# A routed expert layer on one core: the first round starts from what is known beforehand instead of waiting for the round tables

## The reference

```python
w = sel_v / jnp.sum(sel_v, axis=-1, keepdims=True)     # top 2 of the best group of 4
gates = jnp.sum(one_hot(sel_i, 16) * w[..., None], axis=1)
for e in range(16):
    h = silu(x @ w_exp_gate[e]) * (x @ w_exp_up[e])    # 1024 -> 512
    y = y + gates[:, e:e + 1] * (h @ w_exp_down[e])    # 512 -> 1024
```

## Time and profile before

| | us |
|---|---|
| median of 3 runs | 1483.75 |
| lowest and highest run | 1483.48, 1492.34 |
| span of the profiled execution | 1481.6 |
| PE busy (share of the span) | 1413.4 (95%) |
| DVE busy | 598.1 (40%) |
| ACT busy | 273.3 (18%) |

### The profile page before, as it was taken

How to read it: one execution, slowest core, us unless ns; L and a number is a source line. 1 busy time by engine, 2 the same in 40 slices (tenths; PEclk the granted TensorE clock), 3 DMA queues, 4 the chain that set the end, 5 groups by cost and what they waited for, 6 DMA issues and landing times.

```text
span 1481.6 us, 20595 instructions
## 1 busy us (share of the span) xinstructions
PE 1413.4 (95%) x7002; PEld 734.0 (50%) x7002; DVE 598.1 (40%) x1216; ACT 273.3 (18%) x667; POOL 116.8 (8%) x137
## 2 busy tenths in 40 slices
PE   7999998998999999998999999999989999999898
PEld 3787446453344443443457874475543444443344
DVE  5086785545310110106530867844543101101356
ACT  1201335212100100011121013442121101100111
POOL 2100000110000000003000000001100000000300
PEclk9999999999999999999999999988999999999999
DMA  8714003354499999948031240033434999999821
GB/s 298 262 62 155 17 1 118 142 191 155 142 421 426 427 427 426 389 159 291 0 130 58 73 156 5 1 118 142 190 142 143 355 426 427 426 427 427 332 90 47
DMA packets 80941, 319.47 MB, mean 216 GB/s; under 512 B 12684, under 2 KB 15044, under 8 KB 56300
## 3 DMA queue, kind: packets, MB, share of 16 engines
q1 hardware_dynamic: 66772, 272.19, 47.1%
q0 software_dynamic: 9280, 29.68, 5.4%
q10 hardware_dynamic: 4824, 16.75, 2.8%
HBM read 429.21 MB, written 29.67 MB: 310 GB/s over the span
## 4 chain that ended last, share of the span: by engine, by line
PE 82%; DMA 5%; DVE 5%; issue 2%; ACT 2%; SPq 1%; DVEq 1%; POOL 1%; ACTq 0%; POOLq 0%
PE psum L1367 19%; PE psum L957 12%; PE psum L1394 9%; PE psum L1453 8%; PE psum L1025 8%; PE psum L1230 7%; PE psum L927 4%; DMA region<-in_w_exp_up_dram 3%; PE psum L896 2%; PE psum L1368 2%; PE psum L875 2%; PE psum L1281 1%; PE psum L1346 1%; PE psum L1010 1%; PE psum L1047 1%
## 5 line engine op out<-in xcount | busy, mean ns | idle before, releaser
L1367 PE MATMUL psum<-ring,xT 128*64 128x512 f32 x800 | 356.7, 598 | 7.4 <-issue 3.1
L1368 PE MATMUL psum<-region,xT 128*64 128x512 f32 x800 | 357.6, 599 | 0.0
L1367 PEld LDWEIGHTS psum<-ring,xT 128*64 128x64 f32 x800 | 107.4, 138 | 208.8 <-issue 208.7
L1394 PE MATMUL psum<-ring,region 128*64 128x512 f32 x400 | 176.2, 592 | 4.3 <-issue 2.7
L957 PE MATMUL psum<-xT,ring 128*128 128x272 f32 x768 | 176.5, 393 | 0.0
L1395 PE MATMUL psum<-region 128*64 128x512 f32 x400 | 176.3, 593 | 0.0
L957 PEld LDWEIGHTS psum<-xT,ring 128*128 128x128 f32 x768 | 145.8, 190 | 30.1
L2242 DVE COPY region<-psum 128x512 f32<-128x512 f32 x23 | 15.9, 691 | 317.5 <-PE psum L1395 317.5
L1025 PE MATMUL psum<-ring,xT 128*128 128x512 f32 (+1 forms) x288 | 132.5, 603 | 0.6 <-DVE region L1896 0.6
L1453 PE MATMUL psum<-ring,xT 128*128 128x512 f32 x256 | 118.0, 617 | 1.6 <-ACT xT L1495 1.5
L782 POOL TENSOR_TENSOR rr<-rq,half 128x1 f32<-128x1 f32 (+4 forms) x41 | 55.9, 1363 | 723.7 <-DVE rq L1762 267.6
(11 more groups left out here) (286 smaller groups left out, 1464.8 us busy)
## 6 DMA issues: line engine op xcount, KB each, us to landing
region<-in_w_exp_gate_dram SPq DMA_DIRECT2D x54, 1024.0 KB
ring<-in_w_exp_gate_dram SPq DMA_DIRECT2D x54, 1024.0 KB
region<-in_w_exp_up_dram SPq DMA_DIRECT2D x54, 1024.0 KB
ring<-in_w_exp_up_dram SPq DMA_DIRECT2D x54, 1024.0 KB
ring<-in_w_exp_down_dram SPq DMA_DIRECT2D x54, 1024.0 KB
region<-in_w_exp_down_dram SPq DMA_DIRECT2D x54, 1024.0 KB
ring<-in_w_in_dram SPq DMA_DIRECT2D x24, 1024.0 KB, 8.0
expert_results<-region ACTq DMA_DIRECT2D x23, 512.0 KB, 7.7
```

The lines of the kernel that those rows point to most:

```text
L1367: pe.matmul(bank[b][front, :], xeT[:, kc, front], ring[:, BLOCK_SLOT[u], kc % 4, :], start=kc == 0, stop=kc == KC - 1)
L1368: m = pe.matmul(bank[b][last, :], xeT[:, kc, last], back[:, UNIT_ROOM[u], kc % 4, :], start=kc == 0, stop=kc == KC - 1)
L1394: pe.matmul(bank[5 + half][front, :], hT[:, 2 * n + q, front], ring[:, BLOCK_SLOT[u], 2 * q + half, :], start=n + q == 0, stop=n + q == 2)
```

## The change

SP no longer serves round 0 from the tables: the early loads are taken as its weights. The back lane's `down` load moves ahead of the wait for `routed`, and `part_of(gate, 1)` is the first thing that reads the tables. To make that right, experts 0 and 15 always get at least one half tile (`least`, a maximum with 64 rows). The count of rounds done, `base`, is kept in registers by each engine instead of being read from `ctl`, and PE, ACT and DVE wait for `routed` and read `mid` after round 0's rows have been turned and copied. DVE's table arithmetic keeps sizes in rows instead of half tiles, with about as many instructions.

The constants and the table arithmetic:

```diff
-    c["rounds"] = np.stack([r, -1 - r])[None].astype(np.float32)
+    c["rounds"] = np.stack([r, -r])[None].astype(np.float32)
...
+    least = np.zeros(NE)
+    least[[0, NE - 1]] = HALFROWS
...
-                ve.tensor_scalar(R(18, 16, 32), R(18, 16, 32), STEP64, 1.0 / HALFROWS, ALU.subtract, ALU.mult)
+                ve.scalar_tensor_tensor(R(18, 16, 32), R(18, 16, 32), STEP64, tie[:, 32:48], ALU.subtract, ALU.max)
...
-                ve.tensor_scalar(ctl[0:1, 1:2], cumf[0:1, 1:2], -1.0, None, ALU.add)
-                ve.tensor_copy(ctl[0:1, 0:1], cumf[0:1, 0:1]).then_inc(routed, 1)
-                ve.tensor_tensor(cumf[0:1, 0:1], cumf[0:1, 0:1], cumf[0:1, 1:2], ALU.add)
...
+                ve.tensor_scalar(ctl[0:1, 1:2], cumf[0:1, 1:2], -1.0, None, ALU.add).then_inc(routed, 1)
```

SP:

```diff
                 base = rounds_done
+                key = ("pp", 4, 1)
+                hold(full[use(key)], taken(l, key) + 1)
+                hold(xe_full, 16 * (base + 1))
                 for n in range(2):
-                    hold(b_full[BLOCK_SLOT[("gate", n)]], 16 * (base + l + 1))
-                    hold(z_full[BLOCK_SLOT[("gate", n)]], 16 * (base + l + 1))
+                    early("down", n, 1)
                 hold(routed, l + 1)
...
-                for name in ("gate", "up", "down"):
-                    if name == "down":
-                        key = ("pp", 4, 1)
-                        hold(full[use(key)], taken(l, key) + 1)
-                        hold(xe_full, 16 * (base + 1))
-                        part_of("gate", 1)
-                        for n in range(2):
-                            early("down", n, 1)
-                    for n in range(2):
-                        if name != "gate":
-                            hold(b_full[BLOCK_SLOT[(name, n)]], 16 * (base + l + 1))
-                            hold(z_full[BLOCK_SLOT[(name, n)]], 16 * (base + l + 1))
-                    if name != "down":
-                        part_of(name, 0, True)
+                part_of("gate", 1)
...
                 rounds_done = base + mid + 1
-                part_of("down", 0)
                 part_of("up", 1)
```

PE:

```diff
-                pe.wait_ge(routed, l + 1)
-                pe.sem_inc(pe_pass, 1)
-                base = pe.value_load(ctl[0:1, 0:1], min_val=0, max_val=MAXROUND * (DEPTH - 1))
-                mid = pe.value_load(ctl[0:1, 1:2], min_val=MINROUND - 1, max_val=MAXROUND - 1)
-
+                base = rounds_done
...
-                    pe.wait_ge(b_full[s], 16 * (base + l + k + 2))
-                    pe.wait_ge(z_full[s], 16 * (base + l + k + 2))
+                    pe.wait_ge(b_full[s], 16 * (base + k + 1))
+                    pe.wait_ge(z_full[s], 16 * (base + k + 1))
...
                 turn_rows(0)
+                pe.wait_ge(routed, l + 1)
+                pe.sem_inc(pe_pass, 1)
+                mid = pe.value_load(ctl[0:1, 1:2], min_val=MINROUND - 1, max_val=MAXROUND - 1)
+                rounds_done = base + mid + 1
                 gate(0)
```

DVE, after the copy of the turned rows:

```diff
                 rows_half(0)
+
+                ve.wait_ge(routed, l + 1)
+                ve.sem_inc(ve_pass, 1)
+                mid = ve.value_load(ctl[0:1, 1:2], min_val=MINROUND - 1, max_val=MAXROUND - 1)
+                rounds_done = base + mid + 1
```

More of the change, by code:

```diff
@@ L342, in encoder_step @@
         rdec = sb("rdec", [P, 4, 4])
-        tie = sb("tie", [P, 32])
+        tie = sb("tie", [P, 48])
         valid = sb("valid", [P, TILES])
@@ L710, in entry, with part_of @@
                     return e.value_load(ctl[0:1, bass.ds(2 + table * MAXROUND + k, 1)], min_val=lo, max_val=hi)
-                def part_of(name, k, first=False):
+                def part_of(name, k):
                     front = bass.ds(l * NE + entry(0, k, 0, NE - 1), 1)
@@ L720, in part_of @@
                         read = {"gate": (gate_read, gate_full), "up": (up_read, up_full), "down": dn_full}[name][n]
[L721 to L722 removed]
+                        hold(read, base + k + 1)
                         e.dma_start(ring[:, s, :, :], weights(name, n, front), cond=new_front).then_inc(b_full[s], 16)
                         e.dma_start(back[:, UNIT_ROOM[(name, n)], :, :], weights(name, n, last), cond=new_last).then_inc(z_full[s], 16)
[L726 to L739 removed]
+                part_of("gate", 1)
                 e.dma_start(lnp_near[:, 0, :], a["ln2_g"][L].to_broadcast([P, D])).then_inc(ln2p_in, 16)
@@ L908, in _ @@
             pe.wait_ge(ident_bias, 16)
+            rounds_done = 0
             for l in range(DEPTH):
@@ L1676, in _ @@
                     projected(t)
-                sc.wait_ge(routed, l + 1)
-                sc.sem_inc(sc_pass, 1)
-                base = sc.value_load(ctl[0:1, 0:1], min_val=0, max_val=MAXROUND * (DEPTH - 1))
-                mid = sc.value_load(ctl[0:1, 1:2], min_val=MINROUND - 1, max_val=MAXROUND - 1)
+                base = rounds_done
                 def rows_half(k):
@@ L1708, in _ @@
                 rows_half(0)
+                sc.wait_ge(routed, l + 1)
+                sc.sem_inc(sc_pass, 1)
+                mid = sc.value_load(ctl[0:1, 1:2], min_val=MINROUND - 1, max_val=MAXROUND - 1)
+                rounds_done = base + mid + 1
                 silu(0)
@@ L2191, in _ @@
                 ve.drain()
-                ve.tensor_scalar(seat[:, 1, :], rounds[:, 1, :], tiles, cumf[0:1, 1:2], ALU.add, ALU.max)
+                ve.tensor_scalar(seat[:, 1, :], rounds[:, 1, :], rt[0:1, 12, 40:41], cumf[0:1, 1:2], ALU.add, ALU.max)
                 ve.drain()
```

28 lines of the change are left out of this document (13 added, 15 removed).

## The result

The changed kernel takes 1472.79 us (median of 20 runs, 1468.75 to 1483.05) against 1480.53 (20 runs of the kernel before beside it, 1474.64 to 1493.63). The ratio is 0.9948 with a 95% interval of 0.9925 to 0.9971: 0.5% shorter, so a real gain, inside the 1% (14.8 us) that the forecast called what a measurement can tell. Timed again beside other kernels it gave 0.9931 (0.9895 to 0.9967).

A forecast was written before the change was run, and what follows sets the result against it. PE, busy nearly everywhere, was taken to bound the 1481.6 us span. Starts and clock 3.5 (layer 0) and 3.3 us (layer 1) plus SP's lead 4.0 made 10.8: span 1470.8, plus 2.15 to the median, 1473 us; range 1467 to 1480.

The forecast's parts named there:

- signs that the prediction had named itself: Wrong if layer 0's rounds end under 5 or over 8 us earlier, or stretches outside the rounds differ by over 2.
- Transposes earlier: Start of rounds: first transposes no longer wait for PE's two `ctl` reads; 1.8 us in layer 0, 1.6 in layer 1.
- the floor now is the gather: First transposes of each layer: the gathered rows' landing limits their start, so no more than 1.8 and 1.6 us can come.
- The read of `mid`: Behind the first transposes: one read, about 0.95 us, stays hidden on PE, so `gate(0)` starts 1.7 us after the first transpose.
- side sum of 10.9 against 9.9: Total gain in us if the `mid` read is hidden behind queued work (10.9), or if it is not (9.9).
- The clock of `gate(0)`: Shorter rest before the transposes keeps PE's clock up: `gate(0)` 6.9 us instead of 8.6, gain 1.7 us a layer.
- SP's lead: Load queue: SP issues round 2's `gate` 8.8 us earlier in PE's time; worth 4.0 us over both layers, bounds 0 to 8.
- (b): Late rounds: the stretch with full DMA engines starts from a smaller backlog; 2.0 us in layer 0, 1.1 in layer 1.
- (a): Layer 0, `gate(2)`: PE's 0.75 us wait for the load's second half goes, some 0.9 us with the step around it.
- reads in series (2): Start of rounds: register reads do not hide behind the transposes, costing 0.5 us a layer, 1474 us; chance 0.18.
- The clock of another stretch (4): Layer 1, 992 to 1009 us: the low-clock stretch may run up to 7 us shorter, giving 1466 to 1470; chance 0.14.
- The loss of SP's worth (3): Clock falls anyway (1476) or SP's lead is worth nothing, 4.0 us less (1477), both 1480; chance 0.15 in all.

The follow-up runs named there:

- the second profile: The changed kernel, unaltered, profiled a second time: span 1468.2 us, against 1473.9 in its first profile and 1481.6 before the change.
- experiment 6: Changed kernel plus sixteen identity transposes during TensorE's wait for seat tables, and VectorE's `mid` read behind its matrices: 1471.00 us; with the transposes alone 1473.18 us.
- Experiment 1: Changed kernel with SP's load queue put back as before, TensorE again counting round 0's conditional loads, computing engines in the new order: 1483.64 us, ratio to before 1.0028.
- experiment 2: Changed kernel's SP queue kept, but computing engines wait for the tables and read two numbers before the first transposes, as before: 1480.78 us, ratio to before 1.0002.
- Experiment 3: Computing engines changed, load queue as before, but `gate` and `up` of round 0 wait for one signal less: 1481.36 us, ratio to before 0.9989.
- experiment 4: Changed kernel with twelve more table reads on SP ahead of its loop of rounds: 1472.07 us, ratio to before 0.9974.
- experiment 5: Changed kernel without the stores of the rounds' results; total not comparable; layer 0 from `turn_last` to the end 277.01 us against 282.40.

## Why the prediction was right, and where it was not

The time was hit (1473 against 1472.79), but not for all of its reasons. The base of 1483.75 was the median of three runs, 3.2 us above that of the 20 beside the changed kernel; the difference was forecast at 10.8 us and is 7.7, in the medians and in the first pair of profiles. The base was 3.2 us too high and the gain 3.1 us too large, and the two cancel: that the time was hit to 0.2 us is luck. By signs that the prediction had named itself it fails: the rounds of layer 0 end 4.93 and 4.86 us earlier (666.91 to 661.98 and 662.05) where less than 5 was to mean wrong, and outside start and rounds the second profile differs by 6.8 us where over 2 was. The first true `gate` issue comes 0.9 us after TensorE has read half of `gate(1)` (393.31 for 388.94 + 3.44), not within 0.5.

- **Transposes earlier**: 9.06 to 8.14 us in layer 0 (7.44 in the second profile) and 8.75 to 7.07 in layer 1 (8.07 in the second), forecast 1.8 and 1.6. The mechanism is right. In layer 0 of the first profile and layer 1 of the second the floor is the bank's copy (370.15 + 0.59 in layer 0), since the last `pp` products ran partly at the low clock; then only 0.9 and 0.7 us come. The term took the copy from a profile in which it was early, and "the floor now is the gather" holds only then.
- **The read of `mid`**: on TensorE hidden; `gate(0)` starts 1.41 us after the first transpose in place of the forecast 1.7. On VectorE 0.42 us of it are in series, of which 0.2 us a layer reach TensorE (experiment 6). The page Advanced Engine Details and Errata of the Trainium skill, section Sequencer Loop, says that other engine instructions can be read and queued while a control instruction executes. The trace agrees on TensorE (1.41 us), and on VectorE only in part (0.42 us in series). The prediction's side sum of 10.9 against 9.9 does not fit its own total: 10.8, and 9.8 for the rival that costs 0.5 us a layer.
- **The clock of `gate(0)`**: 8.59 and 8.72 us to `turn_last`, forecast 8.7. The number is right and the reason wrong. I gave it to the shorter rest ahead of the transposes. Experiment 1 has, in layer 0, the short rest and the low clock, experiment 2 the long rest and the high one. What went was TensorE's wait for the signal of a skipped load, which I had read in the earlier trace rows (0.53 us, DMA) and taken to hold a copy. Experiment 3 shows that the signal holds `gate(0)` back (1.42 us after the first transpose without it, 3.24 with it). That the clock follows this wait is borne out by the counts of experiment 2 (none of 20 starts against three of six), and not by a cause that was isolated.
- **SP's lead**: this is the step that failed, "(b) the full stretch starts from a smaller backlog", 2.0 us and 1.1 in layer 1. The 0.95 us at `gate(2)` came (a). Of (b) nothing is seen: the waits of the late rounds of layer 0 were 5.1 us above a round and are 5.4, those of layer 1 4.4 and are 5.9. SP was ahead as forecast (393.31 for 404.48, 11.2 us). But a load can be issued only when TensorE frees its slot, so the DMA engines were not full between loads: 363, 410 and 398 GB/s in the three stretches from 404 to 471 us, against 427 when full. By 494 us the changed kernel has moved 39.57 - 37.24 = 2.33 MB more since its first true load, 5.5 us at 427 GB/s: half of the 11.2 us is gone. TensorE itself is 4.4 us earlier at round 3 (432.06 for 436.45) and gains 0.09 us more in each round, so about 1 us of lead is left, about what the first late round varies by from profile to profile (22.69 to 23.62 us with the changed queue, experiment 4 apart). The other two late rounds take 24.1 and 25.4 us before, with the change and in all but two of the other kernels that keep their stores. I had counted the backlog of before and not the holes of after. The backlog itself was counted 0.6 us too large: 404.48 + 61.4 is 465.9, 1.3 us behind 464.60 and not 2. Experiments 4 and 5 agree: 4.5 us of lead are worth nothing, and without the stores' bytes the late waits are gone. For layer 1, where the waits grew by 1.5 us, no experiment was made.
- **Not foreseen**: a round takes 22.36 us in place of 22.45. It goes with the queue's half of the change, in which the counting of the waits ahead of the products is simpler, `base + k + 1` for `base + l + k + 2`: experiment 2 has both, experiments 1 and 3 neither. Whether it is the counting or something else in that half was not tested. That is 1.1 us in the twelve rounds of layer 0's loop, of which the late waits take back 0.3.
- **The sum**: starts 2.7 + 3.4 = 6.1 us (forecast 6.8), from `turn_last` on 284.10 - 282.40 = 1.7 in layer 0 and 260.18 - 260.82 = -0.6 in layer 1, together 1.1 (4.0), outside 0.5: 7.7.
- **The rivals**: reads in series (2) is in part true on VectorE. The clock of another stretch (4) did not tip in the first profile. It did in the second: 3.4 us at the low clock in layer 1's mixing in place of 17.1, and 6.3 us less outside start and rounds (898.2 to 891.9). It goes with the groups of the runs, with about the forecast price: 1471 against 1476 to 1479. The loss of SP's worth (3) is what happened, and it gives back 3 of its 4 us.

The two halves of the change don't add: alone they change start and rounds by -0.2 and -4.6 us, together by -7.2 (-6.6 in the second profile). Both rest on one place, where TensorE waits for what SP signals. Part of these differences is the clock's: experiment 1 lost 1.7 us to it in layer 0.

## What to carry to other kernels

A conditional load that is skipped still costs its consumer a wait until the issuing queue has come to it; a row that blames a DMA which moved nothing is the queue's own lateness, and here reading the tables later on the waiting engine alone gained nothing. In this kernel the queue's lead counted up to the point where the next load is bound by its slot coming free, and no further; price a lead by the holes it leaves too, not only by the backlog it removes. When a median rests on three runs and the kernel has groups of runs 6 us apart, state which group the base is from.

## What the runs showed of the hardware

- A read of a table number into a register by TensorE, about 0.95 us on an idle engine (half of the 1.92 us of two), is hidden behind eight transposes: `gate(0)` starts 1.41 us after them with it and 1.44 without (experiment 2). On VectorE 0.42 us of such a read stay.
- A conditional load that is skipped takes its queue 0.07 to 0.11 us, and its signal still comes only when the queue has reached it: TensorE waited 2.11 and 1.86 us for it in experiment 1.
- The granted clock did not follow the rest ahead of the transposes alone: 2.63 us of rest and full clock (experiment 2), 1.10 and 2.11 us around the transposes and half clock (experiment 1, layer 0), 0.94 and 1.86 us and full clock (its layer 1). Low stretches of 3.4, 6.8, 10 and 17 us are in these profiles, and the same instructions have them in one execution and not in another: outside start and rounds the profiles reach from 891.9 to 903.9 us (886.8 without the stores), with no difference in the work but some 1.3 us a layer for fillers. The two ends are the second profile of the changed kernel, with 3.4 us at the low clock in the retention and mixing stages of each layer, and the kernel with sixteen transposes alone, with 17 us in each.
- A stretch in which TensorE was busy 16.79 of 17.10 us ran at 0.51 of the clock to its end (986.8 to 1003.9 us); TensorE worked nearly all of it before the clock rose.
